# Order of the three split products of a K tile: high weights by low input first, then high by high, then low by high

## The chip, the core and the metric

The kernel runs on one core of a Trainium2 chip. The metric is the time of one execution on the device in microseconds; a version is judged by the median of its runs. The profile is that of one execution.

## What is computed

One layer of a decoder trunk, for a prompt of 256 tokens and 8 sample sequences of one token each (264 columns in all), with a model width of 2048 and an FFN width of 5632:

```python
mod = einsum('bd,de->be', silu(c), w_ada) + b_ada        # shift1, scale1, gate1, shift2, scale2, gate2
h = rmsnorm(x, norm1_g) * (1 + scale1) + shift1
q_nsa, kv_nsa, g_nsa, q_dil, kv_dil, g_merge = project(h, w_in)
o_nsa, o_dil, states = mixer(...)                        # compressed, selected, window and dilated attention
y_a = einsum('btk,kd->btd', o_nsa, w_br_nsa)
y_b = einsum('btk,kd->btd', o_dil, w_br_dil)
x = x + gate1 * einsum('btd,de->bte', g_merge[0] * y_a + g_merge[1] * y_b, w_out)
h = rmsnorm(x, norm2_g) * (1 + scale2) + shift2
f = silu(einsum('btd,df->btf', h, w_gate)) * einsum('btd,df->btf', h, w_up)
x = x + gate2 * einsum('btf,fd->btd', f, w_down)
y = rmsnorm(x, normf_g)
```

Everything is float32. The prompt attends within itself, the samples attend to caches of 2048 past positions; the caches' new rows and updated buffers are outputs too.

## The kernel before

All activations lie transposed, features on the 128 partitions and the 264 tokens along the free axis. A big product with a weight matrix is made of output tiles of 128 features, each a sum over K tiles of 128 input features in one PSUM bank. To keep nearly float32's precision at the speed of the rounded type `fp32r`, every operand is split: high = the value rounded to `fp32r`, low = the value minus high, rounded too. The product of a K tile is then three matmuls into the same bank, high weights by high input, high weights by low input and low weights by high input; low by low is left out. Weights are the stationary operand (128 x 128), inputs the moving one (128 x 264).

Each engine has a program written out by hand, in its own order, and the programs meet at counting semaphores; no scheduler moves an instruction. SyncE's queue loads the weights into ring slots. ScalarE casts a chunk to its high half in a separate buffer (L1396 in the projection, `high`, L1663, afterwards). VectorE subtracts and leaves the low half in the slot itself (L1861, and `low`, L2231). The inputs are split in the same way, once, tile by tile (L1410 and L1888, L2226, L2339). TensorE then multiplies, at three places:

- the projection, L903 to L908: a loop over the 51 tiles of the first part of `w_in`, each with 16 K tiles; between two of them stand small other pieces of work (rotations, turns into token-major order, steps of the adaLN product, L787);
- `split_products`, L1225: used by `merge` (eight pairs of output tiles, with the merge gates and the two branch products), by the output product, by `ffn` (gate and up, 11 x 4 chunks of two halves, without the first one) and by `down` (8 x 8 calls of 11 K tiles each). It is called with the places of the low weights in their slot, of the high weights, and of the two lists of input tiles `x_high`, `x_low`;
- `both_halves`, L1282: the first chunk of the FFN, where the two halves are taken together for each K tile, because its inputs come one by one from VectorE.

At the start of a stage, when the input tiles are only being made, TensorE waits for each K tile's low part (`n1_low`, `x_low`, `m_low`, `h_low`, `f_low`) ahead of its three products. Afterwards it waits once for each chunk, for the low weights (`w_low`, `mg_low`, `wo_low`, `ff_low`, `dn_low`). The last of the three products of the last K tile, low weights by high input, carries the signal on which ScalarE evacuates the bank and overwrites the high buffer of an earlier chunk, and through that VectorE, the loads of SyncE and the cache copies of GpSimd go on.

Of the kernel before, what the change touches and what calls it, by code (L numbers as in the profile page):

```python
# [186 lines left out]
def program(nc, i_, o_, ctx, seen):  # L187
# [220 lines left out]
    x_low = tiles_at((hT0, KT), (oN0, 12))  # L408
# [12 lines left out]
    def half_tile(a):  # L421
        return piece(a, T, F32R)[:, :]
# [318 lines left out]
    def _(pe):  # L741
# [130 lines left out]
        for n in range(NT + 2):  # L872
            if 10 <= n < 14:
                if n == 10:
                    pe.wait_ge(*dve_.at("vpairs"))
                    pe.wait_ge(*act_.at("tm", 6))
                kv = (n - 10) // 2
                both = kTcP[:, 2 * kv:2 * kv + 2, :].rearrange("p s (n l) -> p l s n", l=8)
                for l in range(4 * (n % 2), 4 * (n % 2) + 4):
                    last = mm(bank[6][:, kv * 32:(kv + 1) * 32], w1p[:, kv, l, :, :].rearrange("p j e -> p (j e)"),  # L880
                              both[:, l], start=(l == 0), stop=(l == 7))
                if n == 13:
                    last.then_inc(*pe_.mark("hid", "p"))
            if n == 16:
                pe.wait_ge(*act_.at("gelu", "p"))
                for h in range(2):
                    mm(bank[7][h * DH:(h + 1) * DH, 0:NBP], w2[0:64, 0, :], pgl[0:64, h, 0:NBP], start=True, stop=True)
                for base in (0, DH):
                    for h in range(2):
                        last = mm(bank[6][base:base + 2 * NBP, P + h * DH:P + (h + 1) * DH], pgv[0:64, 2 * NBP * h:2 * NBP * (h + 1)],  # L890
                                  w2[0:64, 1, :], start=True, stop=True)
                last.then_inc(*pe_.mark("kvc", "p"))
            if n < NT:
                kind = TILES[n][0]
                m = 48 if n == 0 else P
                pe.wait_ge(*dve_.at("w_low", n))
                if n >= 3:
                    pe.wait_ge(*act_.at("raw", n - 3))
                w_high, w_low = chunk_piece(chunk_high(n), n, F32R), chunk_piece(chunk_low(n), n, F32R)
                out = bank[acc_bank(n)][0:m, 0:T]  # L900
                if n == 2:
                    pe.wait_ge(*act_.at("kvc", B - 1))
                for k in range(KT):  # L903
                    if n == 0:
                        pe.wait_ge(*dve_.at("n1_low", k))
                    mm(out, w_high[:, k, :], half_tile(n1_high[k]), start=(k == 0), stop=False)  # L906
                    mm(out, w_high[:, k, :], half_tile(n1_low[k]), start=False, stop=False)  # L907
                    last = mm(out, w_low[:, k, :], half_tile(n1_high[k]), start=False, stop=(k == KT - 1))  # L908
                last.then_inc(*pe_.mark("acc", n))
            if n in STEP_OF_TILE:  # L910
                ada(STEP_OF_TILE[n])
            if n - 1 in ROW_OF_TILE:
                ada_turn(ROW_OF_TILE[n - 1])
            if n == 0:
                sample_kv(B - 1)
            if n == 1:

                pe.wait_ge(*act_.at("raw", 0))
                for q in range(QT):
                    turn(bank[6][:, q * 48:(q + 1) * 48], tmp[0:48, 0, q * P:(q + 1) * P], ident[0:48, 0:48])  # L920
                turn(bank[6][0:B, 128:176], tmp[0:48, 0, TP:T], ident[0:48, 0:48]).then_inc(*pe_.mark("gateT"))
            if n == 3:
                pe.wait_ge(*act_.at("gateS"))
                pe.wait_ge(const_rest, 16)
                mm(bank[4][:, 0:48], const("rowsel")[0:B, :], gates8[0:B, :], start=True, stop=True)\
                    .then_inc(*pe_.mark("gateS"))
            if 1 <= n <= NT:
                rope(n - 1)
            if n >= 2:
                token_major(n - 2)  # L930
# [294 lines left out]
        def split_products(out, a, high, f, k_tiles, x_high, x_low, start, stop, tiles_ready=None, first_tile=0):  # L1225
# [3 lines left out]
            for k in range(first_tile, len(x_high)):  # L1229
                if tiles_ready is not None:  # L1230
                    pe.wait_ge(*dve_.at(tiles_ready, k))
                mm(out, w_high[:, k, :], half_tile(x_high[k]), start=(start and k == first_tile), stop=False)  # L1232
                mm(out, w_high[:, k, :], half_tile(x_low[k]), start=False, stop=False)  # L1233
                last = mm(out, w_low[:, k, :], half_tile(x_high[k]), start=False, stop=(stop and k == len(x_high) - 1))  # L1234
            return last

# [45 lines left out]
        def both_halves(s):  # L1282
# [3 lines left out]
            for k in range(KT):  # L1286
                pe.wait_ge(*dve_.at("h_low", k))
                for f in range(2):
                    out = bank[2 * s + f][:, 0:T]
                    mm(out, w_high[f][:, k, :], half_tile(h_high[k]), start=(k == 0), stop=False)  # L1290
                    mm(out, w_high[f][:, k, :], half_tile(h_low[k]), start=False, stop=False)
                    last = mm(out, w_low[f][:, k, :], half_tile(h_high[k]), start=False, stop=(k == KT - 1))
                    if k == KT - 1:
                        last.then_inc(ff_half, 1)
# [1163 lines left out]
```

## Time and profile before

| | |
|---|---|
| Median of three runs | 1966.83 us |
| Lowest, highest of the runs | 1960.11 us, 1966.86 us |
| Span of the profiled execution | 1965.0 us |
| TensorE busy with matmuls | 1870.2 us, 95% |
| VectorE busy | 963.5 us, 49% |
| ScalarE busy | 750.3 us, 38% |
| HBM traffic over the span | 309 GB/s |
| Mean granted clock of TensorE | 0.979 |

The profile gives no time of its own execution beside the span, which runs from the first to the last instruction. A matmul is pipelined with its neighbours, so its duration in the profile is longer than its distance to the next one; a weight load runs beside the matmul ahead of it.

### The profile page before, as it was taken

How to read it: one execution, taken by the hardware profiler on the slowest of the kernel's cores; microseconds unless marked ns; L12 is line 12 of the kernel's file. 1: busy time of each engine (PE TensorE's matmuls, PEld its weight loads, DVE VectorE, ACT ScalarE, POOL GpSimd, SP SyncE). 2: the span in 40 equal slices, each digit the busy share in tenths (PEclk: the TensorE clock that was granted, in tenths of full speed). 3: DMA queues.
4: the chain of work that ended last, by engine and by line, in shares of the span. 5: the costliest groups of instructions: out<-in, count | busy, mean ns of one | idle time of the engine just before them, and what ended most of it. 6: DMA issues, size and time to landing. Idle time of an engine off the chain costs nothing.

```text
span 1965.0 us, 35795 instructions
## 1 busy us (share of the span) xinstructions
PE 1870.2 (95%) x15435; PEld 1713.1 (87%) x15435; DVE 963.5 (49%) x1552; ACT 750.3 (38%) x1101; POOL 58.3 (3%) x108
## 2 busy tenths in 40 slices
PE   5987999999998888999999989999999999999997
PEld 3556899999964555999999989999999999999996
DVE  2437345545346723554446675443444433654454
ACT  2437333333434433533334344333333333633332
POOL 0000000000000000000000000000000000000000
PEclk9999999999999989899999989999999999999999
DMA  8991877886599947987878857777778887688881
GB/s 361 394 378 72 273 237 219 243 239 182 147 388 420 414 164 260 308 270 230 252 244 272 288 201 257 265 280 271 272 257 266 274 286 235 218 289 289 278 279 44
DMA packets 336548, 516.79 MB, mean 263 GB/s; under 512 B 8913, under 2 KB 310265, under 8 KB 319657
## 3 DMA queue, kind: packets, MB, share of 16 engines
q1 hardware_dynamic: 316306, 370.69, 56.7%
q0 software_dynamic: 5248, 125.73, 16.3%
q10 hardware_dynamic: 14896, 18.96, 3.6%
q8 instruction: 74, 1.21, 0.3%
q14 instruction: 24, 0.20, 0.0%
HBM read 506.45 MB, written 101.07 MB: 309 GB/s over the span
## 4 chain that ended last, share of the span: by engine, by line
PE 86%; DMA 7%; DVE 4%; ACT 2%; issue 1%; SPq 0%; ACTq 0%; DVEq 0%
PE bank L1232 19%; PE bank L1233 19%; PE bank L1234 18%; PE bank L906 5%; PE bank L907 5%; PE bank L908 5%; PE bank L787 4%; DMA piece<-in_w_ada 3%; PE bank L824 2%; DMA mem<-in_cache_win_kv 1%; PE bank L813 1%; DMA mem<-in_x_sample 1%; PE bank L855 1%; DMA piece<-in_w_in 1%; DMA x_kept<-mem 1%
## 5 line engine op out<-in xcount | busy, mean ns | idle before, releaser
L1232 PE MATMUL bank<-piece,piece 128*128 128x264 f32 x3040 | 864.4, 284 | 2.4 <-DVE piece L2226 1.5
L1233 PE MATMUL bank<-piece,piece 128*128 128x264 f32 x3040 | 865.4, 285 | 0.0
L1234 PE MATMUL bank<-piece,piece 128*128 128x264 f32 x3040 | 863.8, 284 | 0.0
L2231 DVE TENSOR_TENSOR piece<-piece,piece 128x2048 fp32r<-128x2048 f32 (+2 forms) x216 | 441.0, 2053 | 473.2 <-ACT piece L1663 473.2
L1663 ACT CAST piece<-piece 128x2048 fp32r<-128x2048 f32 (+2 forms) x216 | 369.1, 1716 | 548.7 <-PE bank L1234 498.8
L1232 PEld LDWEIGHTS bank<-piece,piece 128*128 128x128 f32 x3040 | 572.9, 188 | 3.1 <-DVE piece L2231 3.1
L1234 PEld LDWEIGHTS bank<-piece,piece 128*128 128x128 f32 x3040 | 573.2, 189 | 0.0
L1233 PEld LDWEIGHTS bank<-piece,piece 128*128 128x128 f32 x3040 | 572.4, 188 | 0.0
L906 PE MATMUL bank<-piece,piece 128*128 128x264 f32 (+1 forms) x816 | 237.9, 291 | 0.0
L907 PE MATMUL bank<-piece,piece 128*128 128x264 f32 (+1 forms) x816 | 232.0, 284 | 0.0
L908 PE MATMUL bank<-piece,piece 128*128 128x264 f32 (+1 forms) x816 | 231.8, 284 | 0.0
L1396 ACT CAST piece<-piece 128x2048 fp32r<-128x2048 f32 (+1 forms) x51 | 96.2, 1886 | 204.5 <-PE bank L908 199.6
L906 PEld LDWEIGHTS bank<-piece,piece 128*128 128x128 f32 (+1 forms) x816 | 152.7, 187 | 1.4
L907 PEld LDWEIGHTS bank<-piece,piece 128*128 128x128 f32 (+1 forms) x816 | 152.7, 187 | 0.6
L908 PEld LDWEIGHTS bank<-piece,piece 128*128 128x128 f32 (+1 forms) x816 | 152.5, 187 | 0.0
L1861 DVE TENSOR_TENSOR piece<-piece,piece 128x2048 fp32r<-128x2048 f32 (+1 forms) x51 | 115.5, 2266 | 72.9 <-ACT piece L1396 72.8
L787 PE MATMUL bank<-piece,mem 128*32 128x512 f32 x768 | 101.2, 649 | 16.5 <-DMA piece<-in_w_ada 15.7
L1885 DVE COPY mem<-bank 64x256 f32<-64x256 f32 x128 | 54.0, 422 | 63.6 <-PE bank L813 60.4
L787 PEld LDWEIGHTS bank<-piece,mem 128*32 128x32 f32 x768 | 21.4, 114 | 60.4 <-issue 42.3
L824 PE MATMUL bank<-mem 128*128 128x256 f32 x256 | 61.3, 394 | 7.0 <-DVE mem L1885 3.8
L1967 DVE TENSOR_TENSOR mem<-bank,mem 128x264 f32<-128x264 f32 x35 | 15.1, 433 | 105.4 <-PE bank L855 105.4
L1407 ACT COPY mem<-bank 64x256 f32<-64x256 f32 x128 | 46.9, 367 | 49.8 <-PE bank L813 47.3
(345 smaller groups left out, 1362.9 us busy)
## 6 DMA issues: line engine op xcount, KB each, us to landing
piece<-in_w_ada SPq DMA_DIRECT2D x48, 2048.0 KB, 16.1
out_s_dil<-in_cache_dil_kv POOLq DMA_DIRECT2D x64, 1023.5 KB, 6.3
piece<-in_w_in SPq DMA_DIRECT2D x50, 1024.0 KB, 5.8
piece<-in_w_gate SPq DMA_DIRECT2D x22, 2048.0 KB, 9.3
piece<-in_w_up SPq DMA_DIRECT2D x22, 2048.0 KB, 8.4
piece<-in_w_down SPq DMA_DIRECT2D x32, 1408.0 KB, 7.0
piece<-in_w_in SPq DMA_DIRECT2D x16, 2048.0 KB, 8.8
piece<-in_w_out SPq DMA_DIRECT2D x8, 2048.0 KB, 8.5
```

The costliest lines, as they stand in the source:

```text
L787: last = mm(ada_banks(part_)[0][32 * j:32 * j + 32, :], siluP[:, step * ADA_K + k, :], ada_block(a)[:, k, j * 512:(j + 1) * 512], start=(s ...
L824: last = mm(bank[0][:, kv * 256:(kv + 1) * 256], w1p[:, kv, l, :, :].rearrange("p j e -> p (j e)"), both[:, l], start=(l == 0), stop=(l == 7))
L906: mm(out, w_high[:, k, :], half_tile(n1_high[k]), start=(k == 0), stop=False)
L907: mm(out, w_high[:, k, :], half_tile(n1_low[k]), start=False, stop=False)
L908: last = mm(out, w_low[:, k, :], half_tile(n1_high[k]), start=False, stop=(k == KT - 1))
L1232: mm(out, w_high[:, k, :], half_tile(x_high[k]), start=(start and k == first_tile), stop=False)
L1233: mm(out, w_high[:, k, :], half_tile(x_low[k]), start=False, stop=False)
L1234: last = mm(out, w_low[:, k, :], half_tile(x_high[k]), start=False, stop=(stop and k == len(x_high) - 1))
L1396: cp(chunk_piece(chunk_high(n), n, F32R), chunk_piece(chunk_low(n), n, F32)).then_inc(*act_.mark("w_high", n))
L1663: cp(half_chunk(buffer, k_tiles), raw).then_inc(done, 1)
L1861: v.tensor_tensor(chunk_piece(a, n, F32R), chunk_piece(a, n, F32), chunk_piece(chunk_high(n), n, F32R).bitcast(F32), ALU.subtract).then_in ...
L2231: v.tensor_tensor(half_chunk(a, k_tiles, f, CW), raw, half_chunk(buffer, k_tiles).bitcast(F32), ALU.subtract)\
```

## The change

In each of the three places the first two products of a K tile change places. `start`, which clears the bank's sum, goes with the first position; the wait ahead of the three and the third product with its signal stay.

```diff
--- before.py
+++ after.py
@@ -903,8 +903,8 @@
                 for k in range(KT):
                     if n == 0:
                         pe.wait_ge(*dve_.at("n1_low", k))
-                    mm(out, w_high[:, k, :], half_tile(n1_high[k]), start=(k == 0), stop=False)
-                    mm(out, w_high[:, k, :], half_tile(n1_low[k]), start=False, stop=False)
+                    mm(out, w_high[:, k, :], half_tile(n1_low[k]), start=(k == 0), stop=False)
+                    mm(out, w_high[:, k, :], half_tile(n1_high[k]), start=False, stop=False)
                     last = mm(out, w_low[:, k, :], half_tile(n1_high[k]), start=False, stop=(k == KT - 1))
                 last.then_inc(*pe_.mark("acc", n))
             if n in STEP_OF_TILE:
@@ -1229,8 +1229,8 @@
             for k in range(first_tile, len(x_high)):
                 if tiles_ready is not None:
                     pe.wait_ge(*dve_.at(tiles_ready, k))
-                mm(out, w_high[:, k, :], half_tile(x_high[k]), start=(start and k == first_tile), stop=False)
-                mm(out, w_high[:, k, :], half_tile(x_low[k]), start=False, stop=False)
+                mm(out, w_high[:, k, :], half_tile(x_low[k]), start=(start and k == first_tile), stop=False)
+                mm(out, w_high[:, k, :], half_tile(x_high[k]), start=False, stop=False)
                 last = mm(out, w_low[:, k, :], half_tile(x_high[k]), start=False, stop=(stop and k == len(x_high) - 1))
             return last
 
@@ -1287,8 +1287,8 @@
                 pe.wait_ge(*dve_.at("h_low", k))
                 for f in range(2):
                     out = bank[2 * s + f][:, 0:T]
-                    mm(out, w_high[f][:, k, :], half_tile(h_high[k]), start=(k == 0), stop=False)
-                    mm(out, w_high[f][:, k, :], half_tile(h_low[k]), start=False, stop=False)
+                    mm(out, w_high[f][:, k, :], half_tile(h_low[k]), start=(k == 0), stop=False)
+                    mm(out, w_high[f][:, k, :], half_tile(h_high[k]), start=False, stop=False)
                     last = mm(out, w_low[f][:, k, :], half_tile(h_high[k]), start=False, stop=(k == KT - 1))
                     if k == KT - 1:
                         last.then_inc(ff_half, 1)
```

What TensorE has in a row now, by the order written out for both versions. A `piece` is a region of the memory, `bank<-a,b` a matmul that streams `a` and has `b` as its weights. The numbers of the pieces come from the order in which the program first names them, so the same tile has another number in the version after: the rows of VectorE tell which is which, since the piece that it writes there is the low tile and the piece that it reads beside `mem` the high one.

TensorE at the first tile of the projection (48 gate columns). Before:

```order
L906 MATMUL bank<-piece_1511,piece_1508 48x264
L907 MATMUL bank<-piece_1513,piece_1508 48x264
L908 MATMUL bank<-piece_1511,piece_1509 48x264
L906 MATMUL bank<-piece_1517,piece_1508 48x264
L907 MATMUL bank<-piece_1519,piece_1508 48x264
L908 MATMUL bank<-piece_1517,piece_1509 48x264
```

and after:

```order
L906 MATMUL bank<-piece_1511,piece_1508 48x264
L907 MATMUL bank<-piece_1513,piece_1508 48x264
L908 MATMUL bank<-piece_1513,piece_1509 48x264
L906 MATMUL bank<-piece_1517,piece_1508 48x264
L907 MATMUL bank<-piece_1519,piece_1508 48x264
L908 MATMUL bank<-piece_1519,piece_1509 48x264
```

VectorE where it makes the low parts of the same inputs, before:

```order
L1888 TENSOR_TENSOR piece_1513<-mem,piece_1511 128x264
L1888 TENSOR_TENSOR piece_1519<-mem,piece_1517 128x264
L1888 TENSOR_TENSOR piece_1525<-mem,piece_1523 128x264
L1888 TENSOR_TENSOR piece_1531<-mem,piece_1529 128x264
L1888 TENSOR_TENSOR piece_1537<-mem,piece_1535 128x264
```

and after:

```order
L1888 TENSOR_TENSOR piece_1511<-mem,piece_1513 128x264
L1888 TENSOR_TENSOR piece_1517<-mem,piece_1519 128x264
L1888 TENSOR_TENSOR piece_1523<-mem,piece_1525 128x264
L1888 TENSOR_TENSOR piece_1529<-mem,piece_1531 128x264
L1888 TENSOR_TENSOR piece_1535<-mem,piece_1537 128x264
```

Before, piece_1513 is the first low input tile, and L907 streams it; after, piece_1511 is, and L906 streams it. The high input, piece_1511 before and piece_1513 after, has gone to L907 and stays at L908. The weights are piece_1508 (high), twice, and piece_1509 (low), as before.

TensorE at the first FFN chunk (`both_halves`), where L2339 of VectorE writes the same two regions. Before:

```order
L1277 MATMUL bank<-mem 128x264
L1290 MATMUL bank<-piece_1511,piece_6227 128x264
L1291 MATMUL bank<-piece_1513,piece_6227 128x264
L1292 MATMUL bank<-piece_1511,piece_6226 128x264
L1290 MATMUL bank<-piece_1511,piece_6321 128x264
L1291 MATMUL bank<-piece_1513,piece_6321 128x264
L1292 MATMUL bank<-piece_1511,piece_6226 128x264
L1290 MATMUL bank<-piece_1517,piece_6227 128x264
```

and after:

```order
L1277 MATMUL bank<-mem 128x264
L1290 MATMUL bank<-piece_1511,piece_6227 128x264
L1291 MATMUL bank<-piece_1513,piece_6227 128x264
L1292 MATMUL bank<-piece_1513,piece_6226 128x264
L1290 MATMUL bank<-piece_1511,piece_6321 128x264
L1291 MATMUL bank<-piece_1513,piece_6321 128x264
L1292 MATMUL bank<-piece_1513,piece_6226 128x264
L1290 MATMUL bank<-piece_1517,piece_6227 128x264
```

Here too piece_1511 is the high tile before and the low tile after, so for each half (piece_6227 and piece_6321 are the high weights) the low input is now streamed first. The wait stands ahead of the first L1290 in both.

## Rows read from the trace of the kernel before

**Rows 1.** The page's busy times and slices (tenths of 40 equal slices).

```profile
PE 1870.2 (95%) x15435; PEld 1713.1 (87%) x15435; DVE 963.5 (49%) x1552; ACT 750.3 (38%) x1101; POOL 58.3 (3%) x108
...
PE   5987999999998888999999989999999999999997
...
DVE  2437345545346723554446675443444433654454
ACT  2437333333434433533334344333333333633332
...
PEclk9999999999999989899999989999999999999999
```

**Rows 2.** The page's chain that ended last, by engine and by line.

```profile
PE 86%; DMA 7%; DVE 4%; ACT 2%; issue 1%; SPq 0%; ACTq 0%; DVEq 0%
PE bank L1232 19%; PE bank L1233 19%; PE bank L1234 18%; PE bank L906 5%; PE bank L907 5%; PE bank L908 5%; PE bank L787 4%; DMA piece<-in_w_ada 3%; PE bank L824 2%; DMA mem<-in_cache_win_kv 1%; PE bank L813 1%; DMA mem<-in_x_sample 1%; PE bank L855 1%; DMA piece<-in_w_in 1%; DMA x_kept<-mem 1%
```

**Rows 3.** The page's costliest groups: count, busy us, mean ns, idle before.

```profile
L1232 PE MATMUL bank<-piece,piece 128*128 128x264 f32 x3040 | 864.4, 284 | 2.4 <-DVE piece L2226 1.5
L1233 PE MATMUL bank<-piece,piece 128*128 128x264 f32 x3040 | 865.4, 285 | 0.0
L1234 PE MATMUL bank<-piece,piece 128*128 128x264 f32 x3040 | 863.8, 284 | 0.0
...
L1232 PEld LDWEIGHTS bank<-piece,piece 128*128 128x128 f32 x3040 | 572.9, 188 | 3.1 <-DVE piece L2231 3.1
L1234 PEld LDWEIGHTS bank<-piece,piece 128*128 128x128 f32 x3040 | 573.2, 189 | 0.0
L1233 PEld LDWEIGHTS bank<-piece,piece 128*128 128x128 f32 x3040 | 572.4, 188 | 0.0
L906 PE MATMUL bank<-piece,piece 128*128 128x264 f32 (+1 forms) x816 | 237.9, 291 | 0.0
L907 PE MATMUL bank<-piece,piece 128*128 128x264 f32 (+1 forms) x816 | 232.0, 284 | 0.0
L908 PE MATMUL bank<-piece,piece 128*128 128x264 f32 (+1 forms) x816 | 231.8, 284 | 0.0
```

**Rows 4.** Groups by line of TensorE, shapes apart, for `both_halves`.

```profile
L1290 PE MATMUL bank<-piece,piece 128*128 128x264 f32 x32 | 10.2, 320 | 5.8 <-DVE piece L2339 5.8
L1291 PE MATMUL bank<-piece,piece 128*128 128x264 f32 x32 | 10.0, 312 | 0.0
L1292 PE MATMUL bank<-piece,piece 128*128 128x264 f32 x32 | 9.9, 310 | 0.0
```

**Rows 5.** Timeline of a dense stretch of the FFN: start, us, engine, line.

```profile
1500.14 0.28 PE L1232 MATMUL bank<-piece,piece 128*128 128x264 f32 x1
1500.14 0.19 PEld L1233 LDWEIGHTS bank<-piece,piece 128*128 128x128 f32 x1
1500.26 0.29 PE L1233 MATMUL bank<-piece,piece 128*128 128x264 f32 x1
1500.26 0.19 PEld L1234 LDWEIGHTS bank<-piece,piece 128*128 128x128 f32 x1
...
1500.38 0.28 PE L1234 MATMUL bank<-piece,piece 128*128 128x264 f32 x1
...
1503.79 0.28 PE L1232 MATMUL bank<-piece,piece 128*128 128x264 f32 x1
```

**Rows 6.** Stage table: length, busy us and count by engine, granted clock, DMA.

```profile
core 0: us, PE busy (x) PEld busy (x) DVE busy (x) ACT busy (x) POOL busy (x), PEclk, DMA share, GB/s
830.00:930.00 100.00, 100.00 (x828) 100.00 (x827) 44.74 (x36) 37.34 (x34) 1.50 (x3) 1.00 0.77 237
1420.00:1680.00 260.00, 260.00 (x2137) 260.00 (x2136) 105.69 (x71) 90.38 (x71) 10.23 (x21) 1.00 0.78 261
1700.00:1800.00 100.00, 100.00 (x823) 100.00 (x822) 55.94 (x70) 37.53 (x36) 4.38 (x9) 1.00 0.80 271
1820.00:1940.00 120.00, 120.00 (x986) 120.00 (x985) 54.10 (x58) 38.27 (x28) 4.38 (x9) 1.00 0.65 223
```

**Rows 7.** Waits of TensorE by line: total us, times, longest.

```profile
PE bank L1290 <- DVE piece L2339: 5.8, 1, 5.8
...
PE bank L1232 <- DVE piece L2226: 1.5, 1, 1.5
...
PE bank L1232 <- DVE piece L2231: 0.9, 2, 0.7
```

**Rows 8.** Timeline of TensorE at the first projection tile.

```profile
196.16 1.03 PE L824 MATMUL bank<-mem 128*128 128x256 f32 x4
196.83 0.47 PE L906 MATMUL bank<-piece,piece 128*48 128x264 f32 x1
197.14 0.28 PE L907 MATMUL bank<-piece,piece 128*48 128x264 f32 x1
197.26 0.28 PE L908 MATMUL bank<-piece,piece 128*48 128x264 f32 x1
197.38 0.28 PE L906 MATMUL bank<-piece,piece 128*48 128x264 f32 x1
```

**Rows 9.** Timeline of TensorE at the first FFN tile.

```profile
1167.67 0.42 PE L1292 MATMUL bank<-piece,piece 128*128 128x264 f32 x1
1167.89 0.42 PE L1290 MATMUL bank<-piece,piece 128*128 128x264 f32 x1
1168.11 0.42 PE L1291 MATMUL bank<-piece,piece 128*128 128x264 f32 x1
```

**Rows 10.** Stage table of 4 us at the first FFN tile; columns as in rows 6.

```profile
1167.00:1171.00 4.00, 3.91 (x18) 3.94 (x19) 4.00 (x11) 2.65 (x6) 0.00 (x0) 0.50 0.00 0
```

## The prediction, made before the changed kernel was run

> **What bounds the kernel now.** I read the views from coarse to fine. The page's busy times come first: TensorE's matmuls are busy 1870.2 us of the 1965.0 us span, and the slice rows show them at 9 tenths in most slices, with VectorE and ScalarE at a third to a half [rows 1]. The chain that ended last agrees: 86% of it is TensorE, and the six lines of split products in the page's list take 19 + 19 + 18 + 5 + 5 + 5 = 71% of the span [rows 2]. So whatever the three products of a K tile cost is paid in the end time, and nearly nothing else is on the path in those stages. The groups of instructions give the counts: 3040 of each line of `split_products`, 816 of each projection line, 32 of each line of `both_halves` [rows 3, 4]: 3888 K tiles, 11,664 products, each with a weight load of its own.
>
> A matmul's "mean ns of one" (284) is a latency with its neighbours overlapped, so it is not the price. The price is the distance between starts. In a dense stretch the first starts at 1500.14 us and the thirtieth after it at 1503.79 [rows 5]: 3.65 / 30 = 121.7 ns. The stage table says the same with other counts: 2137 matmuls in 260 us of the FFN are 121.7 ns each, 986 in 120 us and 823 in 100 us of the down product 121.7 and 121.5 ns, and only the merge stage is a little quicker, 828 in 100 us, 120.8 ns [rows 6]; since a window counts two or three instructions that only reach into it, a value is good to about 0.3 ns. 11,664 x 121.7 ns = 1419.5 us, or 72% of the span, which meets the chain's 71%.
>
> **Part 1: nothing is added or removed.** Each K tile has the same three matmuls of 264 columns and the same three weight loads before and after. Cost by count: 0 us.
>
> **Part 2: the waits.** The wait for the low input tile stands ahead of all three products in both versions, and so does the wait for the split weights. Before, the high input was multiplied first, though its low partner had to be there as well; so reading the low tile first does not make TensorE wait earlier or longer. Had the wait stood between the first and the second product, the new order would cost one product's lead per waited tile; here it costs 0. What these waits take is small in any case: 5.8 us ahead of L1290, 1.5 + 0.9 us ahead of L1232 [rows 7]. The last product of a K tile is in both versions the low weights by the high input, and it carries the signal that frees the bank, the weight buffers and ScalarE's next split. Its place is unchanged, so ScalarE's casts, VectorE's subtractions, the loads of SyncE and the copies of GpSimd that wait for it are released at the same position in TensorE's stream. 0 us.
>
> **Part 3: the first product of a tile after other work.** L906 has a mean of 291 ns where L907 and L908 have 284 [rows 3]. The reason is in the timeline: the first L906 of a projection tile is 0.31 us ahead of its L907 instead of 0.12 [rows 8]. That sits on the position behind the other kind of matmul (the FP32 products of L824 there), not on which input it reads; 51 such places stay as they are. 0 us; the bound, if it went or doubled, is (291 - 284) ns x 816 = 5.7 us either way.
>
> **Part 4: what stands next to what.** This is all that really changes. While one product streams its input, the next product's weights are loaded (the load rows start with the matmul before them) [rows 5]. Before, the three neighbours in a K tile are: high input streaming with the high weights loading again; low input with low weights loading; high input with the next K tile's high weights loading. After, they are: low input with high weights; high input with low weights; high input with the next high weights. Two of the three pairings are new, 7776 of 11,664. No row shows these two, so I bound them. In the trace the three lines, with three different pairings, have latencies of 284, 285 and 284 ns and loads of 188, 188 and 189 ns [rows 3]: the pairing hardly matters. Between stages, where the tiles lie at other places of the memory and the traffic differs, the distance moves by 121.7 - 120.8 = 0.9 ns [rows 6]. If both new pairings moved by all of that, it would be 7776 x 0.9 ns = 7.0 us, up or down. I take 0, since the rows of the three lines, which are the nearest to the question, stand within 1 ns of each other, in no order that follows from reading high or low.
>
> Does the chip gain where two products share an operand? Before, the first two share the high weights, and the load in front of L1233 still takes 188 ns, 3040 times [rows 3]: the repeated load is not skipped. After, the first two still share the weights, and now the second and third also share the input. As the shared weights give nothing, I expect nothing of the shared input. The Trainium skill ("TensorE: Matmul & The Clock Gate", on what happens when a matmul is issued) says that TensorE has separate read ports for the streamed operand and for the weights, so loading does not take bandwidth from the running matmul; by that rule the pairing costs exactly nothing and the sum is the same 0 us. The same page, in its section on the back-to-back gap, gives the distance as columns over the clock plus 2.5 ns; an estimate from it is 112.5 ns for 264 columns, and here the trace disagrees, with 121.7 ns, so something beside streaming does set the pace.
>
> The trace itself shows that remainder. At a granted clock of 0.50, that is 1.2 GHz, [rows 10] the products stand 0.22 us apart [rows 9], which is 264 columns at one a cycle. At 1.00, 2.4 GHz, streaming would be half of it, 110 ns, but the distance is 121.7: 11.7 ns per product come from something that I can't name. It is the only room in which an order could gain or lose much, and it is where both rivals below live.
>
> **The sum.** 0 + 0 + 0 + 0 us on a profiled span of 1965.0 us. The page gives no time of that execution beside its span; the median of the three runs is 1966.83 us, 1.8 us more, which lies around the span. So the forecast is **1966.8 us**, no change. Its own bound is 7.0 us for the pairings, and the three runs shown already spread from 1960.11 to 1966.86. About 0.5% (9.8 us) is what a measurement of this kernel can tell from no change.
>
> **Rivals.**
> *Faster: sharing the input pays.* If the third product could use what the second has just streamed, or the second read of the same tile no longer disturbs anything, the 11.7 ns would vanish for one product in three: 3888 x 11.7 ns = 45.5 us, giving 1921 us. For it: the remainder exists, and a doubled input is really new. Against it: the doubled weights, of which the order before has one pair per K tile, show no sign of such a saving [rows 3]. From 2.5 ns per K tile (9.8 us / 3888) it would be visible. 3%.
>
> *Slower: a new pairing collides.* Its place is the distance from the first to the second product or from the second to the third: the low input streams while the high weights load, and the high input streams while the low weights load, and one of these reads meets the other in the memory. The price can't be read from a row; if it is as large as the remainder again, 3888 x 11.7 ns = 45.5 us, giving 2012 us; it decides, again, from 2.5 ns per K tile, or 1.3 ns on each of the two pairings. For it: distances do differ by 0.9 ns from stage to stage [rows 6]. Against it: those are 0.9 ns, not 1.3, between tiles at quite different places. 4%.
>
> *The change does not do what it says.* If the program were put in another order when it is built, time and trace would be those of before. The instruction order written out for both versions shows the new reads in the new places, so 1% for this; its time is also 1966.8.
>
> *Clock.* A different order of the same numbers might draw another current. The granted clock is 1.00 in all the dense stretches [rows 6] and falls to 0.50 only where TensorE has stood idle just before (5.8 us at L1290 [rows 7, 10]). A fall over a dense stage would cost 98 ns per product, and nothing in the change makes TensorE idle. Under 1%, and counted with slower.
>
> **How the numbers follow.** No change: 91%, of which 1 for the program that is the same. Inside 0.5% everything from the pairing bound (7.0 us) fits, unless it falls together with a run-to-run shift of the size that the runs show, and for that I add 1% on the faster and 0 on the slower side. Faster 4%, same 91%, slower 5%. The range: 1966.8 + 7.0 = 1973.8 and about a microsecond for the spread of runs on the upper side gives 1975; 1966.8 - 7.0 = 1959.8 and, as one run in three lay 6.7 us under the median without any change, a little more, 1957. That leaves out the two rivals and some of the tails, well under 2 in 10, and I don't narrow it, since the bound of the unknown pairing is what makes it.
>
> **What would show it right or wrong.** Part 1: the same counts in the groups, 3040, 816 and 32 for each line. Part 2: the idle time ahead of L1290 and L1232 is again 5.8 and about 2.4 us, now with the low tile as the first product's input. Part 3: the extra 7 ns of latency stays at L906 and does not follow the high input to L907. Part 4: 30 products in about 3.65 us in a dense stretch, 2137 within two or three per 260 us in the same stage, and means of 283 to 286 ns for all six lines. If the time were changed, the count in the 260 us stretch would say so: with 11.7 / 3 = 3.9 ns on each product, the faster rival would give 2137 x 121.7 / 117.8 = 2208, the slower one 2137 x 121.7 / 125.6 = 2071. The prediction is wrong if the pace per K tile moves by over 2.5 ns from its 365 ns.

## The result: a quarter of a per cent slower, and where it lies

The changed kernel took a median of 1970.64 us (12 runs, 1966.53 to 1973.68), the kernel before beside it 1965.94 us (12 runs, 1960.11 to 1968.16). The ratio is 1.0024, with a 95% interval of 1.0014 to 1.0034. The time lies inside the range of the prediction, but the forecast "no change" does not stand: the kernel is slower, by 2.8 to 6.7 us, with 4.7 us between the medians.

The page of after has the same counts as [rows 3]. TensorE's busy time is 3.1 us longer, but not line by line: L1232 and L1234 have gained 2.3 and 1.7 us, and L1233 has lost 0.4.

```profile
PE 1873.3 (95%) x15435; PEld 1716.7 (87%) x15435; DVE 963.8 (49%) x1552; ACT 749.8 (38%) x1101; POOL 58.3 (3%) x108
...
L1232 PE MATMUL bank<-piece,piece 128*128 128x264 f32 x3040 | 866.7, 285 | 4.0 <-DVE piece L2226 3.1
L1234 PE MATMUL bank<-piece,piece 128*128 128x264 f32 x3040 | 865.5, 285 | 0.0
L1233 PE MATMUL bank<-piece,piece 128*128 128x264 f32 x3040 | 865.0, 285 | 0.0
...
L906 PE MATMUL bank<-piece,piece 128*128 128x264 f32 (+1 forms) x816 | 238.7, 292 | 0.0
L907 PE MATMUL bank<-piece,piece 128*128 128x264 f32 (+1 forms) x816 | 232.4, 285 | 0.0
```

These means are rounded to a nanosecond and can't carry a difference of 0.1%. The starts in the timeline can. The first and last products of the projection (L906, L908), of the FFN's loop and of down (L1232, L1234) follow. "The FFN's loop" stands here and below for all of the FFN behind `both_halves`: the other products of chunk 0 and the ten passes of the loop, 4128 products. In the kernel before:

```profile
196.83 0.47 PE L906 MATMUL bank<-piece,piece 128*48 128x264 f32 x1
547.40 0.29 PE L908 MATMUL bank<-piece,piece 128*128 128x264 f32 x1
1180.87 0.28 PE L1232 MATMUL bank<-piece,piece 128*128 128x264 f32 x1
1683.41 0.28 PE L1234 MATMUL bank<-piece,piece 128*128 128x264 f32 x1
1683.53 0.28 PE L1232 MATMUL bank<-piece,piece 128*128 128x264 f32 x1
1941.98 0.28 PE L1234 MATMUL bank<-piece,piece 128*128 128x264 f32 x1
```

and in the kernel after:

```profile
195.95 0.47 PE L906 MATMUL bank<-piece,piece 128*48 128x264 f32 x1
548.18 0.28 PE L908 MATMUL bank<-piece,piece 128*128 128x264 f32 x1
1183.23 0.28 PE L1232 MATMUL bank<-piece,piece 128*128 128x264 f32 x1
1687.07 0.28 PE L1234 MATMUL bank<-piece,piece 128*128 128x264 f32 x1
1687.19 0.28 PE L1232 MATMUL bank<-piece,piece 128*128 128x264 f32 x1
1945.14 0.28 PE L1234 MATMUL bank<-piece,piece 128*128 128x264 f32 x1
```

The projection takes 352.23 us after 350.57 (+1.66), the FFN's loop 503.84 after 502.54 (+1.30), down 257.95 after 258.45 (-0.50). Merge behind its first 144 products and the output product, read in the same way, move by less than 0.05 us. The sum is **+2.4 us**. The two spans differ by 3.6 us; the rest came between the stages, most of it at the start of merge. There TensorE waited 3.1 us for VectorE instead of 1.5, and its products stood 220 ns apart right behind the first, as at half clock in [rows 9, 10], where before's slowed to that only some products later; merge's first 144 products took 22.23 us after 21.08. So the stages account for 2.4 of the 4.7 us between the medians, and 2.4 us lies just under the interval of 2.8 to 6.7.

### The profile page after: what moved, and what is told of

Its sections match the earlier page's. It is cut to its first block, busy times and chain, and to the rows that moved or that the text cites. A ratio compares the mean times of both kernels' runs of the same rounds, so it can differ in the third digit from the quotient of the medians.

```text
span 1968.6 us, 35795 instructions
## 1 busy us (share of the span) xinstructions
PE 1873.3 (95%) x15435; PEld 1716.7 (87%) x15435; DVE 963.8 (49%) x1552; ACT 749.8 (38%) x1101; POOL 58.3 (3%) x108
## 4 chain that ended last, share of the span: by engine, by line
PE 87%; DMA 6%; DVE 4%; ACT 2%; issue 1%; SPq 0%; ACTq 0%; DVEq 0%
PE bank L1232 19%; PE bank L1234 19%; PE bank L1233 19%; PE bank L906 5%; PE bank L907 5%; PE bank L908 5%; PE bank L787 4%; PE bank L824 3%; DMA piece<-in_w_ada 2%; DMA mem<-in_cache_win_kv 1%; PE bank L813 1%; PE bank L855 1%; DMA mem<-in_x_sample 1%; DMA piece<-in_w_in 1%; DMA x_kept<-mem 1%; PE bank L1131 1%
## 5 line engine op out<-in xcount | busy, mean ns | idle before, releaser
L1232 PE MATMUL bank<-piece,piece 128*128 128x264 f32 x3040 | 866.7, 285 | 4.0 <-DVE piece L2226 3.1
L1234 PE MATMUL bank<-piece,piece 128*128 128x264 f32 x3040 | 865.5, 285 | 0.0
L1233 PE MATMUL bank<-piece,piece 128*128 128x264 f32 x3040 | 865.0, 285 | 0.0
L1232 PEld LDWEIGHTS bank<-piece,piece 128*128 128x128 f32 x3040 | 573.6, 189 | 4.6 <-DVE piece L2231 4.6
L1233 PEld LDWEIGHTS bank<-piece,piece 128*128 128x128 f32 x3040 | 573.4, 189 | 0.0
L1234 PEld LDWEIGHTS bank<-piece,piece 128*128 128x128 f32 x3040 | 573.3, 189 | 0.0
L906 PE MATMUL bank<-piece,piece 128*128 128x264 f32 (+1 forms) x816 | 238.7, 292 | 0.0
L907 PE MATMUL bank<-piece,piece 128*128 128x264 f32 (+1 forms) x816 | 232.4, 285 | 0.0
L908 PE MATMUL bank<-piece,piece 128*128 128x264 f32 (+1 forms) x816 | 232.2, 285 | 0.0
L906 PEld LDWEIGHTS bank<-piece,piece 128*128 128x128 f32 (+1 forms) x816 | 152.5, 187 | 1.4
L907 PEld LDWEIGHTS bank<-piece,piece 128*128 128x128 f32 (+1 forms) x816 | 152.6, 187 | 0.6
L908 PEld LDWEIGHTS bank<-piece,piece 128*128 128x128 f32 (+1 forms) x816 | 152.4, 187 | 0.0
L1967 DVE TENSOR_TENSOR mem<-bank,mem 128x264 f32<-128x264 f32 x35 | 15.2, 433 | 106.7 <-PE bank L855 106.7
```

What stands on the lines that cost most here:

```text
L906: mm(out, w_high[:, k, :], half_tile(n1_low[k]), start=(k == 0), stop=False)
L907: mm(out, w_high[:, k, :], half_tile(n1_high[k]), start=False, stop=False)
L1232: mm(out, w_high[:, k, :], half_tile(x_low[k]), start=(start and k == first_tile), stop=False)
L1233: mm(out, w_high[:, k, :], half_tile(x_high[k]), start=False, stop=False)
```

## Experiments

The diffs are cut to the lines that matter; changed signatures and calls are mostly left out.

The theory after the result: each stage has a pace that belongs to the order of its products, exactly, and the +2.4 us are the sum. The rival: the differences are chance, like the 7 us over which the runs of either kernel spread.

**1. Control.** The kernel before, unedited.

> The kernel before once more, as a control. If the pace of the products is fixed by the program, each stage has the length of the first trace to within 0.05 us: 350.6 us from the first to the last product of the projection, 46.76 us for each pass of the FFN loop, 502.5 us for the loop's stage, 258.5 us for down; only the DMA-bound stretches around them move. If the pace is a matter of chance or of the chip, these lengths move by about a microsecond, as they do between before (502.5) and after (503.8).

Measured: projection 350.65, FFN loop 502.54, down 258.44 us, and each of its FFN passes 46.76 us, against 350.57, 502.54, 258.45 and 46.76 in the first trace; ratio 1.0004 (0.9991 to 1.0017). Only the projection is off by more than the 0.05 us that I had allowed: 0.08, and in later traces of this order up to 0.3. And the start of merge, in this kernel with the old order:

```profile
PE bank L1290 <- DVE piece L2339: 5.8, 1, 5.8
...
PE bank L1232 <- DVE piece L2226: 3.2, 1, 3.2
```

The wait of 3.2 us is there too, and merge's first 144 products take 22.13 us, so that part of after's span does not belong to the order. Two later kernels with the new order in merge, after_zero_low and after_k_back, wait only 1.7 and 1.8 us there. The stages' lengths are not chance.

**2. The change in one stage at a time.**

```diff
@@ split_products, low_first=True in ffn_only for the FFN loop, in down_only for down
+                first, second = (x_low[k], x_high[k]) if low_first else (x_high[k], x_low[k])
+                mm(out, w_high[:, k, :], half_tile(first), start=(start and k == first_tile), stop=False)
+                mm(out, w_high[:, k, :], half_tile(second), start=False, stop=False)
```

`proj_only` has the first hunk of the change and nothing else.

> Low input first in the projection alone. If the pace belongs to the order within a stage, the projection takes 352.2 us, as in the kernel after (1.66 us more than before), and FFN and down keep 502.5 and 258.5 us; the time rises by about 1.7 us, ratio 1.0008. If the slowdown of after came from somewhere else (a disturbed run, a wait), the projection stays at 350.6 us.

> Low input first in the FFN's loop alone (not in its first chunk). Order theory: the FFN stage takes 503.8 us, 46.88 us a pass in place of 46.76, projection and down as before; 1.3 us slower. Rival (chance): 502.5 us.

> Low input first in down alone. Order theory: down takes 257.95 us, 0.5 us less than before, and the other stages stay; this one would be faster than before by 0.5 us, ratio 0.9998. Rival (any new order costs, since low data is read first): down is longer than 258.5 us.

| us | projection | FFN loop | down | ratio of times |
|---|---|---|---|---|
| before | 350.57 | 502.54 | 258.45 | |
| ctrl | 350.65 | 502.54 | 258.44 | 1.0004 (0.9991 to 1.0017) |
| after | 352.23 | 503.84 | 257.95 | 1.0024 (1.0014 to 1.0034) |
| proj_only | **352.30** | 502.63 | 258.44 | 1.0009 (0.9996 to 1.0022) |
| ffn_only | 350.55 | **503.84** | 258.44 | 1.0018 (1.0003 to 1.0033) |
| down_only | 350.88 | 502.54 | **257.94** | 1.0009 (0.9997 to 1.0022) |

Each edited stage (bold) takes on the length it has in after, and no other does. The loop of `ffn_only`, where the lines stand one lower:

```profile
1181.46 0.28 PE L1233 MATMUL bank<-piece,piece 128*128 128x264 f32 x1
1685.30 0.28 PE L1235 MATMUL bank<-piece,piece 128*128 128x264 f32 x1
```

The order theory holds and chance falls. That down_only's ratio points the other way than its stage shows what the timing can resolve: with a dozen runs the interval is 0.0025 wide, 4.9 us, ten times the effect of 0.5 us that was looked for.

**3. What is shared, or what stands where?** The other four orders, in all big products at once (the edit is shown for one of them, in the projection; hh is high weights by high input, lh low weights by high input, hl high weights by low input):

```diff
@@ order_lh_hh_hl, projection
-                    mm(out, w_high[:, k, :], half_tile(n1_high[k]), start=(k == 0), stop=False)
-                    mm(out, w_high[:, k, :], half_tile(n1_low[k]), start=False, stop=False)
-                    last = mm(out, w_low[:, k, :], half_tile(n1_high[k]), start=False, stop=(k == KT - 1))
+                    mm(out, w_low[:, k, :], half_tile(n1_high[k]), start=(k == 0), stop=False)
+                    mm(out, w_high[:, k, :], half_tile(n1_high[k]), start=False, stop=False)
+                    last = mm(out, w_high[:, k, :], half_tile(n1_low[k]), start=False, stop=(k == KT - 1))
```

> In all big products: low weights by high input, high by high, high by low. The first two share the input, the last two the weights. In the FFN alone this order took 503.06 us. Sharing theory (what is shared decides): every stage comes out as in the kernel after, 352.2, 503.8, 258.0 us for projection, FFN, down, since the same two things are shared. Phase theory: each stage has its own value, FFN again 503.1, projection and down anywhere within 1 ns per product of before.

> Low weights by high input, high by low, high by high. Neighbours share the weights (second and third) and, across the K tile, nothing. Sharing theory: as before in each stage (350.6, 502.5, 258.5 us), where also only the weights were shared. Phase theory: no such tie, differences of up to 2 us a stage either way.

> High by high, low weights by high input, high weights by low input. The weights are never shared inside a K tile, the input is, in the first two. Sharing theory: if shared weights save anything, this is the slowest of all, above 352.2 and 503.8 us in projection and FFN; phase theory: no tie, within 2 us a stage.

> High weights by low input, low by high, high by high. The input is shared by the last two, the weights by none inside the K tile. Sharing theory: the same lengths as for the order high by high, low by high, high by low. Phase theory: not the same.

| us | inputs | projection | merge (behind its first 144 products) | output product | FFN loop | down |
|---|---|---|---|---|---|---|
| hh lh hl | H H L | 350.07 | 239.59 | 93.55 | 501.89 | 258.56 |
| lh hh hl | H H L | 349.92 | 239.21 | 93.62 | 503.08 | 258.53 |
| hh hl lh (before) | H L H | 350.57 | 238.27 | 93.74 | 502.54 | 258.45 |
| lh hl hh | H L H | 350.72 | 239.46 | 93.75 | 502.85 | 258.47 |
| hl hh lh (after) | L H H | 352.23 | 238.23 | 93.73 | 503.84 | 257.95 |
| hl lh hh | L H H | 352.16 | 238.81 | 93.88 | 503.30 | 257.94 |

The sharing theory (what two neighbours share decides) falls: hh hl lh and lh hl hh share the same things and differ by 1.2 us in merge, and the slowest in the projection is the quickest in down. The phase theory (each order has its own sum of small shifts, tied to nothing) is not right either. In the projection and in down the length follows the order in which the *inputs* are streamed, to 0.15 us, whatever the weights; in merge and in the FFN the weights take part. The single times of these four kernels (1960.91, 1963.48, 1965.60 and 1964.97 us, before 1967.04) are one run each and rank nothing.

One of these orders, lh hh hl, had been tried before in the FFN's loop alone, with a slightly different form of the code:

> The order low weights by high input, high by high, high weights by low input in the FFN's loop. It too has two neighbours with the same input and two with the same weights. Sharing theory (a shared input costs, a cost that follows the pair): slower than 502.5 us, near 503.8. Phase theory (each order has its own sum of small shifts): any value from 499 to 506, and not tied to what is shared.

That loop took 503.06 us; with the order in all stages it takes 503.08.

**4. Places or numbers?** Two edits of the kernel after:

```diff
@@ after_zero_low: the low input tiles of the projection are zero
-                v.tensor_tensor(half_tile(n1_low[k]), hT[:, k, :], half_tile(n1_high[k]).bitcast(F32), ALU.subtract)\
+                v.tensor_tensor(half_tile(n1_low[k]), half_tile(n1_high[k]).bitcast(F32), half_tile(n1_high[k]).bitcast(F32), ALU.subtract)\
@@ after_k_back: the projection's K tiles from the last to the first
-                for k in range(KT):
+                ks = list(range(KT)) if n == 0 else list(range(KT))[::-1]
+                for k in ks:
```

> The kernel after, with the low parts of the projection's inputs set to zero (they are left out of the result). Place theory: the projection takes 352.2 us, as in after. Number theory (what is streamed decides): it changes, by a microsecond or more, since a third of all streams is now zeros.

> The kernel after, with the K tiles of the projection taken from the last to the first (all tiles but the first, which must follow the norm). The numbers and products are the same; only which tile stands next to which across a K boundary changes. Place theory: the projection's length moves off 352.2 us by over 0.2 us, and its means by position off 122.5, 122.4, 122.4 ns. If only the order of high and low inside a K tile counts: 352.2 us.

With a third of the streams all zeros the projection takes 352.15 us, against 352.23: these numbers don't matter (zeros in place of the high inputs or of the weights were not tried). With the same products in the opposite order of K it takes 351.25 us, and the mean distances behind the three positions go from 122.5, 122.4, 122.3 ns to 121.5, 121.6, 122.9 (from all starts of the stage, stalls over 150 ns left out). The products and their numbers are the same and only their sequence has changed, so at least here it is which place follows which. First and last product of the projection in after_k_back, whose last line is one lower:

```profile
197.22 0.47 PE L907 MATMUL bank<-piece,piece 128*48 128x264 f32 x1
548.48 0.28 PE L909 MATMUL bank<-piece,piece 128*128 128x264 f32 x1
```

In the FFN's loop I also took the changes of place away:

```diff
@@ ffn_one_input
+                mm(out, w_high[:, k, :], half_tile(h_high[0]), start=(k == 0), stop=False)
+                mm(out, w_high[:, k, :], half_tile(h_high[0]), start=False, stop=False)
+                last = mm(out, w_low[:, k, :], half_tile(h_high[0]), start=False, stop=(k == KT - 1))
@@ ffn_one_weight
+                mm(out, w_high[:, 0, :], half_tile(h_high[k]), start=(k == 0), stop=False)
+                mm(out, w_high[:, 0, :], half_tile(h_low[k]), start=False, stop=False)
+                last = mm(out, w_high[:, 0, :], half_tile(h_high[k]), start=False, stop=(k == KT - 1))
```

`ffn_all_same` takes `w_high[:, 0, :]` by `h_high[0]` in all three.

> All products of the FFN's loop stream the first high input tile (the other tiles and the low input are left out), weights as before. If the fractions of a nanosecond hang on where two neighbouring streams start, the means of the three positions come together and the stage moves off 502.5 us by over 0.3 us; with no jump between streams I expect the lower end, 120.9 ns, 499 us. If they hang on the code or the weights alone, the stage is 502.5 us to within 0.1.

> All products of a chunk half in the FFN's loop take the weights of its first K tile's high half (the low weights are left out), inputs and their order as before. If the place of the weights takes part, the means of the three positions move from 121.5, 122.05, 121.8 by over 0.2 ns; if only the inputs do, they stay and the stage is 502.5 us.

> Every product of the FFN's loop takes the first K tile's high weights and the first high input (all others are left out). If the places make the differences, the three positions have one mean, within 0.1 ns, and the pass differs from 46.65 us, which one input with changing weights took. If the positions keep different means, something besides the places takes part.

Loop 501.45, 502.10 and 501.99 us, a pass 46.65, 46.72 and 46.72. Mean distances by position: 121.0, 121.8, 121.8 ns; 121.1, 121.8, 122.1; 121.7, 121.5, 121.8. Both the inputs' and the weights' places count, as expected; but my lower end, 499 us, is not reached, and even the same product 4128 times keeps a spread: single distances go mostly from 115 to 127 ns in a repeating pattern. Nor do the three positions come to one mean within 0.1 ns, as the place theory asked: 121.7, 121.5 and 121.8 ns are 0.3 apart, as much as the 0.31 ns per changed product that this case is about. So the places shift the pace, but they are not all of it: something besides them takes part. What it is, and what makes the pattern, stays open; the instructions' own places in the program, for one, were not varied.

**5. What holds a product at 121.7 ns.**

The FFN's loop with fewer streamed columns, 128 or, with 256 in place of 128, 256:

```diff
@@ ffn_cols128
+                mm(out[:, 0:128], w_high[:, k, :], half_tile(h_high[k])[:, 0:128], start=(k == 0), stop=False)
+                mm(out[:, 0:128], w_high[:, k, :], half_tile(h_low[k])[:, 0:128], start=False, stop=False)
+                last = mm(out[:, 0:128], w_low[:, k, :], half_tile(h_high[k])[:, 0:128], start=False, stop=(k == KT - 1))
```

> The FFN's loop (not its first chunk) streams 128 of the 264 columns and leaves the others out. If streaming plus a fixed 11.7 ns sets the pace, a product takes 128 / 2.4 + 11.7 = 65 ns and the loop's stage 502.5 x 65 / 121.7 = 268 us or what the casts and loads allow. If the weight load or the issue sets it, a product stays at about 111 ns (the distance of L979's matmuls, 128 weight columns and 128 streamed) to 122 ns, and the stage at 460 to 502 us.

> The FFN's loop streams 256 of the 264 columns (the 8 samples are left out there). If streaming and a fixed part set the pace at 264 columns, a product loses 8 / 2.4 = 3.3 ns, to 118.4 ns, and a pass of the loop takes 45.5 us in place of 46.76. If the weight load sets it, the pass stays at 46.7.

The stage rows (columns as in rows 6) of ffn_cols128 and then of ffn_cols256:

```profile
1220.00:1380.00 160.00, 160.00 (x1435) 160.00 (x1434) 70.66 (x44) 61.31 (x46) 7.30 (x15) 1.00 0.82 293
```

```profile
1220.00:1380.00 160.00, 160.00 (x1357) 160.00 (x1356) 66.11 (x41) 57.43 (x44) 7.03 (x15) 1.00 0.78 276
```

The loop takes 460.79 us with 128 columns and 487.56 us with 256. By the rows, 160 / 1435 = 111.5 ns with 128 columns, 160 / 1357 = 117.9 with 256 (all starts: 111.7 and 118.1), 121.7 with 264. The last eight columns cost 3.6 ns, near the 3.3 of streaming them at 2.4 GHz; the 128 columns before those cost only 6.4 ns together. So there are two limits close to each other. One is streaming with some 11 ns beside it. It holds at 264 columns even where few weights are loaded: the projection's first tile has 48 weight columns, and its products stand 0.12 us apart too [rows 8].

The other, 111.7 ns, is not the issue of instructions. In the kernel before, 32 products with 32 weight columns, which go four at a time to four parts of a bank, take 1.01 us in the chain:

```profile
711.64 1.01 PE bank L1111 x32
```

Nor does it hang on the streamed columns. Two rows of before's timeline have runs of matmuls of other operands, at a granted clock of 1.00. L767 loads 64 weight columns and streams 1, L1222 loads 128 and streams 4:

```profile
37.80 6.96 PE L767 MATMUL bank<-mem 128*64 128x1 f32 x64 [1.21 <-DVE mem L1834]
812.87 1.93 PE L1222 MATMUL bank<-mem 128*128 128x4 f32 x16
```

Without the last one's latency (0.245 and 0.253 us) that is 6.96 - 0.25 over 63 distances, 107 ns, and 1.93 - 0.25 over 15, 112 ns. So a load with its matmul takes 107 to 112 ns even where next to nothing is streamed.

The Trainium skill ("TensorE: Matmul & The Clock Gate", section "LDWEIGHTS (loading the stationary operand)") gives the load as its columns over 1.2 GHz; an estimate from it is 106.7 ns for 128 columns. The run is 5 ns above that. But by the same rule 64 columns would take 53 ns, an estimate too, and L767's matmuls stand 107 ns apart. So the load may be this limit, but that is not shown; in this trace, at least, half the weight columns do not take half the time.

**6. Adding up, and the time of after once more.**

`best_mix` has the projection in the order lh hh hl, and `split_products` takes the order as an argument; merge and the first FFN chunk keep that of before.

```diff
@@ output product
+                                   True, True, "m_low" if n == 0 else None, order="hh lh hl").then_inc(wo_half, 1)
@@ FFN loop
+                                   True, True, order="hh lh hl").then_inc(ff_half, 1)
@@ down
+                                   f"f_low{s}" if very_first and f == 0 else None, order="hl hh lh").then_inc(dn_half, 1)
```

> Each stage in the order that was shortest for it: projection low by high, high by high, high by low; output product and FFN loop high by high, low by high, high by low; down as in the kernel after; merge and the first FFN chunk as before. If the stages are independent, they take 349.9, 93.6, 501.9 and 257.9 us, 2.0 us less than before together, ratio 0.9990. If the start of a stage carries over from the one ahead, the lengths differ from these by over 0.1 us.

> The kernel after once more, on the chip of this call. If the stages are all of it, its time is 2.4 us above before, ratio 1.0012, with an interval that holds 1.0012; stages 352.2, 503.8, 258.0 us. If something else is in the measured 1.0024, the interval lies above 1.0012 again.

best_mix: projection 349.81, output product 93.59, FFN loop 501.85, down 257.94, merge unchanged at 238.27 us: 2.1 us less than before, where the separate runs add up to 2.0. Its median is 1964.03 us, before 1967.01; ratio 0.9988 (0.9973 to 1.0002). The stages are 2.1 us shorter; that the whole is faster, the timing leaves just open.

after_again: 352.05, 503.84 and 257.95 us, and a ratio of 1.0006 (0.9993 to 1.0020), which holds the 1.0012 of the stages. But the interval of the first comparison (1.0014 to 1.0034) just misses 1.0012, and this one just misses 1.0024; they share only 1.0014 to 1.0020. So 2.4 us are shown as the cost of the order. The other 2.3 us of the first comparison did not come back in this one, and their cause stays open.

## Why the prediction was wrong, step by step

**Bound and count** were right: TensorE's products hold 71% of the chain of before, and the counts are the same. **Part 2** held: the wait at L1290 is 5.8 us in before, after and the control, and the move from 2.4 to 4.0 us at L1232 comes in the control as well. **Part 3** held: the longer latency stayed at L906 (292 ns), now with the low input, and L907 has 285. The prediction's later sign "283 to 286 ns for all six lines" contradicts its own Part 3: L906 had 291 ns before.

**Part 4** is the step that failed. It named the right thing, two new neighbourships for 7776 products, and a bound that holds (7.0 us; +2.4 measured, which is 0.31 ns on each of them). But it then took 0, since the three lines' latencies were 284, 285 and 284 ns. That evidence could not bear it. A step of 1 ns on 7776 products is 7.8 us; a row that is rounded to a nanosecond can't tell 2.4 us from nothing. And a latency is not the distance that the prediction itself had called the price. By the starts, before's three neighbourships in the FFN do differ: 121.5, 122.05 and 121.8 ns, always the same. Whether an unseen pairing would cost or gain could not be read from that either, and down's went the other way; the honest term was its own bound, up to 7 us with the sign unknown, and not 0.

Of its signs of being wrong, one showed: 2132 products in the 260 us of the FFN, five fewer than 2137, where it allowed two or three. The other, 2.5 ns on the 365 of a K tile, did not: the projection's 1.66 us are 2.0 ns on each of its 816 K tiles. That threshold came from 0.5% of the whole time and was too coarse for what there was to see.

Its remainder of 11.7 ns, "something that I can't name", it set beside an estimate of 112.5 ns in which the load has no part. Experiment 5 shows a second limit at 111.7 ns, so that near 264 columns streaming is not the only thing that counts; the 11.7 ns themselves stay unexplained.

**"About 0.5% is what a measurement can tell"** was too coarse: a dozen runs of each gave an interval of +-0.1%, and the stage lengths of one order repeat from trace to trace to 0.03 us in down, to 0.1 us in the FFN (a pass of its loop to 0.001) and to some 0.3 us in the projection.

**The rivals.** The slower one, a collision of a new pairing, has the right kind of cause and place, but a price of 45 us where the measured sum is 2.4. The faster one, shared input, falls with the third experiment: the input orders H H L and L H H both share it, and lie 2 us apart in the projection. The clock played no part: in the FFN's 260 us after has 1.00 as in [rows 6], with 2132 products for 2137.

```profile
1420.00:1680.00 260.00, 260.00 (x2132) 260.00 (x2131) 107.05 (x71) 89.27 (x72) 10.21 (x21) 1.00 0.79 264
```

## What to carry to other kernels

An edit that only reorders thousands of equal instructions isn't free by default: ask for the distance between starts over a whole stage, not for a rounded mean, and multiply its last digit by the count before calling it zero. Compare stage lengths in the traces of two versions; in a stage with one full engine they repeat far better than the run's time, which here spreads over 7 us and more. And such small effects add up by stage, so each stage can have its own order, but with the six orders tried here 2 us of 1966 is all there was in it.

## What the runs showed of the hardware that I had not expected

The pace of a dense stretch is exact: every pass of the FFN's loop took 46.76 us with the order of before, in before, the control, `proj_only` and `down_only`, and 46.88 with that of after, also in `ffn_only` and `after_again`, which ran on two different chips. Inside it the distance between products jumps between 115 and 133 ns in a pattern that comes again in each pass, to a nanosecond or so. The order of the three products shifts the pattern's mean by up to 0.9 ns (352.23 - 349.92 us over the projection's 2448 products). The places of the streamed tiles and of the weights take part in that (experiment 4), though not alone; low inputs of zeros changed nothing (352.15 us). And a product of 264 columns lies just above another limit, 111.7 ns, so that 128 columns in their place save only 10 ns of 122; loads with next to nothing streamed behind them stand 107 to 112 ns apart as well, with 64 weight columns or 128.
